# Four edits to a hybrid attention and PEER kernel: a warm-up on GpSimd, a later place for three row gathers, another order of products at two beginnings, residual rows in eight pieces

## The reference

```
proj = x @ w_in                                # GLA and retention inputs
mix  = concat(gla(proj), retention(proj)) @ w_out
h    = layer_norm(ALPHA * x + mix) * ln1_g + ln1_b
q    = h @ w_peer_q                            # 8 heads x 2 x 128
scores = q . subkeys ; top 16 of 128, twice ; top 16 of the 256 sums
act  = gelu(h . u[expert]) * softmax(gate)     # 128 experts a token
out  = layer_norm(ALPHA * h + sum(act * v[expert])) * ln2_g + ln2_b
```

## Time and profile before

| what | value |
|---|---|
| median of 3 runs | 1937.12 us (1935.56 to 1940.14) |
| the profiled execution | 1930.02 us, its span 1928.2 us |
| mean granted TensorE clock | 0.997 |
| PE busy | 1902.5 us, 99% |
| DVE, ACT, POOL busy | 1340.2, 989.5, 1436.9 us |
| DMA moved | 440.60 MB, mean 229 GB/s |

### The profile page before, as it was taken

How to read it: one execution, slowest core, us unless ns; L and a number is a source line. 1 busy time by engine, 2 the same in 40 slices (tenths; PEclk the granted TensorE clock), 3 DMA queues, 4 the chain that set the end, 5 groups by cost and what they waited for, 6 DMA issues and landing times.

```text
span 1928.2 us, 34656 instructions
## 1 busy us (share of the span) xinstructions
PE 1902.5 (99%) x10830; PEld 1664.7 (86%) x10830; DVE 1340.2 (70%) x2305; ACT 989.5 (51%) x1518; POOL 1436.9 (75%) x962
## 2 busy tenths in 40 slices
PE   9999999999999999999999999999999999999996
PEld 8999888888998888888888888888788888888885
DVE  1844012214688877765889998997788888888887
ACT  5544434435445556657455555555555555555553
POOL 6877878887878899989788878786476576666631
PEclk9999999999999999999999999999999999999998
DMA  9555657577869888787977777777899999999983
GB/s 302 174 153 164 205 149 226 176 232 181 212 148 206 185 190 192 166 189 182 251 172 176 173 172 174 167 177 208 305 328 339 333 329 343 357 352 367 359 311 114
DMA packets 197497, 440.60 MB, mean 229 GB/s; under 512 B 29408, under 2 KB 40544, under 8 KB 196272
## 3 DMA queue, kind: packets, MB, share of 16 engines
q1 hardware_dynamic: 181712, 384.40, 69.6%
q0 software_dynamic: 14416, 50.61, 7.6%
q10 hardware_dynamic: 1296, 4.65, 0.7%
HBM read 426.79 MB, written 12.78 MB: 228 GB/s over the span
## 4 chain that ended last, share of the span: by engine, by line
PE 78%; POOL 10%; issue 7%; DMA 3%; DVE 1%; ACT 1%; POOLq 0%; SPq 0%; DVEq 0%; ACTq 0%
PE ps L1817 27%; PE ps L1772 17%; PE ps L1773 9%; PE ps L1512 7%; PE ps L1514 7%; PE ps L1513 7%; POOL u_lo L1429 6%; POOL w_lo L1391 4%; PE ps L1754 3%; DMA v_raw<-in_peer_v 2%; DMA u_raw<-in_peer_u 1%; PE ps L1628 1%; PE ps L1737 0%; DVE u_t L1055 0%; PE ps L1508 0%
## 5 line engine op out<-in xcount | busy, mean ns | idle before, releaser
L1429 POOL TENSOR_TENSOR u_lo<-u_t,u_hi 128x512 fp32r<-128x512 f32 x512 | 653.8, 1300 | 127.5 <-ACT u_hi L637 125.2
L1772 PE MATMUL ps<-xT,u_hi 128*128 128x512 f32 x2048 | 724.3, 397 | 0.6 <-POOL u_lo L1429 0.4
L1773 PE MATMUL ps<-xT,u_lo 128*128 128x256 f32 x2048 | 572.9, 280 | 0.0
L1391 POOL TENSOR_TENSOR w_lo<-raw,w_hi 128x1024 fp32r<-128x1024 f32 x174 | 431.2, 2493 | 99.6 <-ACT w_hi L506 93.2
L637 ACT ACTIVATE u_hi<-u_t 128x512 fp32r<-128x512 f32 x512 | 321.2, 632 | 349.8 <-DVE u_t L1055 348.6
L1772 PEld LDWEIGHTS ps<-xT,u_hi 128*128 128x128 f32 x2048 | 384.2, 188 | 88.2 <-issue 0.9
L1055 DVE STREAM_TRANSPOSE u_t<-u_raw 128x512 f32<-128x512 f32 x512 | 355.5, 702 | 97.5 <-PE ps L1773 60.5
L1773 PEld LDWEIGHTS ps<-xT,u_lo 128*128 128x128 f32 x2048 | 386.7, 189 | 0.0
L506 ACT ACTIVATE w_hi<-raw 128x1024 fp32r<-128x1024 f32 x175 | 184.9, 1059 | 273.7 <-PE ps L1514 261.1
L1454 POOL DMA_INDIRECT sp_rows<-in_peer_v,sp_at x128 | 180.1, 1407 | 152.8 <-DVE far_sum L1268 133.3
L1817 PE MATMUL ps<-v_lo,m_hi 128*128 128x512 f32 x882 | 270.2, 375 | 0.0
(11 more groups left out here) (233 smaller groups left out, 2688.3 us busy)
## 6 DMA issues: line engine op xcount, KB each, us to landing
u_raw<-in_peer_u SPq DMA_DIRECT2D x512, 256.0 KB, 4.8
v_raw<-in_peer_v SPq DMA_DIRECT2D x252, 512.0 KB, 6.2
raw<-in_w_in SPq DMA_DIRECT2D x111, 512.0 KB, 3.8
raw<-in_w_out SPq DMA_DIRECT2D x32, 512.0 KB, 4.8
raw<-in_w_peer_q SPq DMA_DIRECT2D x128, 128.0 KB, 4.3
act_dram<-act_w ACTq DMA_DIRECT2D x4, 1024.0 KB, 6.6
act_dram<-far_act SPq DMA_DIRECT2D x62, 64.0 KB, 5.0
x_again<-in_x SPq DMA_DIRECT2D x1, 2048.0 KB, 8.1
```

The lines of the kernel that those rows point to most:

```text
L1391: pool.tensor_tensor(w_lo[:, k, :], raw[:, k, :], w_hi[:, k % HI_RING, :].bitcast(F32), ALU.subtract).then_inc(lo_done, 1)
L1429: pool.tensor_tensor(u_lo[:, r, :], u_t[:, r, :], u_hi[:, r, :].bitcast(F32), ALU.subtract).then_inc(ulo_done, 1)
L1772: pe.matmul(acc, u_hi[:, r, c], xT[:, :, kt, :], start=kt == 0, stop=False)
L1773: ins = pe.matmul(acc[:, 0:T], u_lo[:, r, c], xT_hi[:, kt, :], start=False, stop=kt == KT - 1)
```

## The change

- **GpSimd**: ahead of the two powers of the last norm, a drain, a multiplication of one column (128x1), a drain and an addition of one column, into a cell that nobody reads.
- **Row gathers**: two (`S_AHEAD`) stand ahead of the activations' gathers instead of five; the other three stand behind the nine `act_gather` of the first chunk.
- **First norm (group 18)**: the first two rows `kt` are turned into two banks. ACT writes each straight to `xT_hi` with gain and bias, and then both again to bank 4, from which DVE makes `xT_lo`. TensorE makes one more turn, then the products high x high and low x high of both rows (`upper_four`), then turns 2 and 3, then the products with `xT_lo` (`lower_four`).
- **Head (group 0)**: `upper_four` of row 0, turn 1, `lower_four` of row 0, and both of row 1.
- **Residual rows**: the two multiplications and two additions are cut in two each, and each of the eight pieces waits for one more step of group 19, `used(O_END + 1, 0)` to `used(O_END + 1, 7)`. `h1_made` is counted behind the sixth and the eighth piece.

```diff
--- before.py
+++ after.py
@@ -53,6 +53,7 @@
 S_CHUNK, S_FIRST = (5, 4), 2
 S_PAIR = sum(S_CHUNK)
 S_SLOTS = S_CHUNK[0]
+S_AHEAD = 2
 S_PAIRS = P // S_PAIR
 LN2_TURN = P // 4 - 1
 UR = 6
@@ -226,6 +227,7 @@
         last_e = small[:, 184:200]
         shift = small[:, 184:186]
         gmax = small[:, 184:200]
+        pool_spare = small[:, 199:200]
         LOW_ROW = 32
         STACK = LOW_ROW + RANK
         wup_sb = wup[0:STACK, :]
@@ -245,6 +247,9 @@
 
         def by_four(row):
             return row.rearrange("p (q t) -> p q t", t=4)
+
+        def first_bank(k):
+            return bank(2 if k else 4)[:, 0:T]
 
         def u_bank(i):
             return bank((0, 1, 7)[i % 3])
@@ -261,6 +266,7 @@
 
         step_free, hi_done, lo_done, acc_free = sem("step_free"), sem("hi_done"), sem("lo_done"), sem("acc_free")
         tr_done, tr_hi, tr_lo = sem("tr_done"), sem("tr_hi"), sem("tr_lo")
+        first_tr, first_hi = sem("first_tr"), sem("first_hi")
         glrw_hi, glrw_lo, glr_done, glrT_done, logit_done = (sem(n) for n in ("glrw_hi", "glrw_lo", "glr_done", "glrT_done", "logit_done"))
         logsig_act, b_done, decay_act, decay_d, decay_done = (sem(n) for n in ("logsig_act", "b_done", "decay_act", "decay_d", "decay_done"))
         lvl_diff, lvl_exp, lvl_ready, lvl_mm, lvl_acc = (sem(n) for n in ("lvl_diff", "lvl_exp", "lvl_ready", "lvl_mm", "lvl_acc"))
@@ -495,6 +501,15 @@
                 act.activation(z, z, ACT.Identity, bias=ln_rows[:, 1, kt:kt + 1], scale=ln_rows[:, 0, kt:kt + 1])
             act.drain()
             act.activation(xT_hi[:, 2 * c:2 * c + 2, :].rearrange("p a b -> p (a b)"), bank(4 + c % 4), ACT.Copy).then_inc(tr_hi, 1)
+
+        def act_first_turn(act):
+
+            for k in range(2):
+                act.wait_ge(first_tr, k + 1)
+                act.activation(xT_hi[:, k, :], first_bank(k), ACT.Identity, bias=ln_rows[:, 1, k:k + 1], scale=ln_rows[:, 0, k:k + 1]).then_inc(first_hi, 1)
+            for k in range(2):
+                ins = act.activation(bank(4)[:, k * T:(k + 1) * T], first_bank(k), ACT.Identity, bias=ln_rows[:, 1, k:k + 1], scale=ln_rows[:, 0, k:k + 1])
+            ins.then_inc(tr_hi, 1)
 
         @block.scalar
         def _(act):
@@ -606,7 +621,8 @@
                 act.wait_ge(sk_mm, c + 1)
                 act.activation(skT[:, 4 * c:4 * c + 4, :].rearrange("p a b -> p (a b)"), bank(4 + c), ACT.Copy).then_inc(sk_sb, 1)
             act.wait_ge(ln1_in, 128)
-            for c in range(4):
+            act_first_turn(act)
+            for c in range(1, 4):
                 act_scaled_turn(act, c)
             for k in range(4, STEPS):
                 hi_steps(O_END, (k,))
@@ -1035,10 +1051,16 @@
 
             dve.wait_ge(ln1_rows_in, 64)
             for a in range(TT):
-                dve.tensor_tensor(part(h1_rows[:, a, :], 0, KT), in_perm(n_perm[:, a, :], 0, KT), part(ln1g_sb[:], 0, KT), ALU.mult)
+                for f in (0, KT // 2):
+                    dve.wait_ge(step_free, used(O_END + 1, 2 * a + f // 8))
+                    dve.tensor_tensor(part(h1_rows[:, a, :], f, KT // 2), in_perm(n_perm[:, a, :], f, KT // 2), part(ln1g_sb[:], f, KT // 2), ALU.mult)
             dve.drain()
             for a in range(TT):
-                dve.tensor_tensor(h1_rows[:, a, :], h1_rows[:, a, :], ln1b_sb[:], ALU.add).then_inc(h1_made, 1)
+                for h in range(2):
+                    c = slice(h * D // 2, (h + 1) * D // 2)
+                    dve.wait_ge(step_free, used(O_END + 1, 4 + 2 * a + h))
+                    ins = dve.tensor_tensor(h1_rows[:, a, c], h1_rows[:, a, c], ln1b_sb[:, c], ALU.add)
+                ins.then_inc(h1_made, 1)
 
 
             def u_quarter(ii, j, f, three=False):
@@ -1459,13 +1481,15 @@
             pool.wait_ge(near_out, 64)
             pool.wait_ge(picks_in, 16)
             pool.wait_ge(uparts_free, UR + 4 * P)
-            for k in range(S_SLOTS):
+            for k in range(S_AHEAD):
                 row_gather(k)
             for s in range(2):
                 pool.wait_ge(far_out[s], 16 * P // 4)
             pool.dma_start(sp_gate[:], gate_dram).then_inc(gate_in, 16)
             for k in range(S_PAIR):
                 act_gather(k)
+            for k in range(S_AHEAD, S_SLOTS):
+                row_gather(k)
             for k in range(S_SLOTS, P):
                 row_gather(k)
                 if k - S_SLOTS + S_PAIR < P:
@@ -1483,6 +1507,10 @@
                 pool.drain()
                 pool.tensor_tensor(o, o, ln2b_sb[:, c], ALU.add).then_inc(y_pool, 1)
 
+            pool.drain()
+            pool.tensor_tensor(pool_spare, sp_gate[:, 0:1], sp_gate[:, 1:2], ALU.mult)
+            pool.drain()
+            pool.tensor_tensor(pool_spare, sp_gate[:, 0:1], sp_gate[:, 1:2], ALU.add)
             ln_power(3, slice(0, 1))
             last_gain(0, 2, 1)
             ln_power(4, slice(1, 2))
@@ -1541,6 +1569,22 @@
                                         kt == 0 and n % 2 == 0, kt == KT - 1, lint=True)
                     ins.then_inc(step_free, 1)
 
+            def upper_four(g, kt):
+
+                for w in (w_hi, w_lo):
+                    for n in range(4):
+                        c = slice(kt * COL + n * P, kt * COL + (n + 1) * P)
+                        o = ps[:, 2 * (g % 2) + n // 2, (n % 2) * T:(n % 2 + 1) * T]
+                        pe.matmul(o, w[:, 0, c], xT_hi[:, kt, :], start=kt == 0 and w is w_hi and n % 2 == 0, stop=False, skip_group_check=True)
+
+            def lower_four(g, kt):
+
+                for n in range(4):
+                    c = slice(kt * COL + n * P, kt * COL + (n + 1) * P)
+                    o = ps[:, 2 * (g % 2) + n // 2, (n % 2) * T:(n % 2 + 1) * T]
+                    ins = pe.matmul(o, w_hi[:, 0, c], xT_lo[:, kt, :], start=False, stop=False, skip_group_check=True)
+                return ins
+
             def steps_t(g, ks=range(STEPS)):
 
                 for k in ks:
@@ -1577,7 +1621,17 @@
             pe.wait_ge(keep_in, 16)
             ready = lambda c: (x_in[c // 2] if c else x_half, 16)
             turn(x_sb, 0, 0, *ready(0))
-            for k in range(STEPS):
+            acc_wait(0)
+            pe.wait_ge(lo_half, 1)
+            pe.wait_ge(tr_hi, 1)
+            upper_four(0, 0)
+            turn(x_sb, 0, 1, *ready(1))
+            pe.wait_ge(tr_lo, 1)
+            lower_four(0, 0)
+            pe.wait_ge(lo_done, 1)
+            upper_four(0, 1)
+            lower_four(0, 1).then_inc(step_free, 1)
+            for k in range(1, STEPS):
                 pe.wait_ge(tr_lo, k + 1)
                 if k < 2:
                     steps_n(0, (k,), between=lambda: turn(x_sb, 0, k + 1, *ready(k + 1)))
@@ -1724,7 +1778,30 @@
             pe.wait_ge(acc_free, freed(O_END))
             keep_busy(bank(0)[:, 0:T], xT_hi[:, KT - 1, :], 8)
             pe.wait_ge(sk_sb, 4)
-            turned_group(O_END, steps_n, n_perm, 2, lambda c: (n_block, 2 * c + 2 if c < 2 else 2 * (c // 2) + 4), lead=4)
+            blocks = lambda c: (n_block, 2 * c + 2 if c < 2 else 2 * (c // 2) + 4)
+            pe.wait_ge(*blocks(0))
+            for k in range(2):
+                for a in range(TT):
+                    ins = pe.transpose(first_bank(k)[:, a * P:(a + 1) * P], by_tile(n_perm, a, k), ident)
+                ins.then_inc(first_tr, 1)
+            pe.sem_inc(tr_done, 1)
+            turn(n_perm, 2, 1, *blocks(1))
+            pe.wait_ge(lo_done, STEPS * O_END + 1)
+            for kt in range(2):
+                pe.wait_ge(first_hi, kt + 1)
+                upper_four(O_END, kt)
+            for c in (2, 3):
+                turn(n_perm, 2, c, *blocks(c))
+            pe.wait_ge(tr_lo, 17)
+            for kt in range(2):
+                ins = lower_four(O_END, kt)
+            ins.then_inc(step_free, 1)
+            turn(n_perm, 2, 4, *blocks(4))
+            for k in range(1, STEPS):
+                pe.wait_ge(tr_lo, 16 + k + 1)
+                steps_n(O_END, (k,))
+                if k + 4 < 8:
+                    turn(n_perm, 2, k + 4, *blocks(k + 4))
 
             def query_scores(n):
 
```

## The result

The changed kernel takes **1948.24 us** (median of 6 runs, 1944.63 to 1953.60), the kernel before 1935.89 beside it (1933.08 to 1940.14). The ratio is 1.0063, 95% interval 1.0049 to 1.0077: 12.3 us slower. The forecast was 1946.5, a step of +9.4 from a median of 1937.1.

What follows compares the result with a forecast made beforehand. The prediction took the kernel to be bound by TensorE's own work. Stand +13.1, clock +2.4, values -2.0 and tail -4.1 gave +9.4, added to the median 1937.1: 1946.5 us, range 1940 to 1954.

Steps and rivals of the forecast that it cites:

- Residual rows and their queue: Before group 20: last piece waits for group 19's end, delaying store and loads; TensorE stands 15.1, ends 13.1 later.
- Rival A: Residual rows are not held, pieces run under group 18 and the store is early: 1929.0, faster; chance 0.07.
- GpSimd's wait gone: Group 19, about 493: eight pieces of 1.2 each remove TensorE's wait of 0.7 for GpSimd's w_lo.
- The clock: In the new stand before group 20, TensorE's clock falls from 2.4 to 1.2 GHz, costing 2.4.
- rival D: Clock doesn't fall in the stand before group 20, or comes back sooner: 1944.1; chance 0.09.
- The cover of 2.4 at DVE: DVE's routing starts 18 late, TensorE 13 to 16; the second wait of its kind, 2.4, covers the rest.
- Norm: First norm, group 18: ACT writes xT_hi directly, so upper products start sooner; gain 1.2.
- Start: Group 0: upper products start earlier but transposes wait for x's second part; step 0 ends at 10.7; gain 0.1.
- Values: Expert values' beginning, about 1357: three row gathers leave the full DMA stretch, removing TensorE's 1.70 stall; gain 2.0.
- Rival C: The value phase gives its gain of 2.0 back, its DMA engines staying above 0.9: 1948.5; chance 0.12.
- Tail: After the last matmul: GpSimd's warm-up moves the 4.19 idle before its first addition into earlier waiting; gain 4.1.
- Rival B: The 4.19 idle in the tail is the drain behind a power, which the change keeps: 1950.6; chance 0.26.

Runs made afterwards that it cites:

- the kernel with ScalarE's store: Kernel before plus new norm order, three rows behind, pieces gated four steps earlier, one drain as warm-up, h1_rows store issued by ScalarE: 1925.95 us against 1932.46.
- the kernel with whole rows: Changed kernel with residual rows made as before, in two multiplications and two additions without waits for group 19: 1927.58 us against 1933.40 for the kernel before.

## Why the prediction was right

The main step held: the last piece waits for the end of group 19, the store for it, and the loads of group 20 for the store. The number is nearer than the working. 1946.5 lies 1.7 below what was measured, but the forecast step was +9.4 and the measured one +12.3 (+9.5 to +14.9 by the interval); 1.2 of the 2.9 between them were hidden because the kernel before came out at 1935.9 and not at 1937.1. That was luck. Point by point, by its own steps:

- **Residual rows and their queue: right.** Issue at 508.5 forecast, 510.3 in the trace; ScalarE's first load of group 20 at 518.85 forecast, 521.25 in the trace; stand 15.1 forecast, 16.0 measured. The 1.8 by which the store was late is the start, which came out 1.9 late where I had a gain of 0.1; the other 0.6 is the load, which took 10.9 behind the store and not 10.3. Alone the pieces cost 17.7, and taking them back returns 18.1 (12.3 + 5.8). Rival A (rows not held) is out.
- **GpSimd's wait gone: right**, 0.9 against 0.7. The pieces took 1.7 to 3.0 beside GpSimd and 1.23 only once it stood idle; I had 1.2 for all. The sum did not suffer, because only the last one counts, and that one is alone. The Trainium skill (SBUF — State Buffer, section SBUF: two separate sides) says that of a DVE operation with two inputs in SBUF and a GpSimd operation that reads SBUF, whichever starts first locks the other out for its whole instruction. 1.23 alone against 3.3 beside GpSimd, in the kernel with ScalarE's store, agrees.
- **The clock: right in size, wrong in kind.** 2.7 against 2.4, and rival D (no fall) is out. But a sum of terms overstates it: with the clock held up, TensorE waited 3.3 for `u_lo` instead, since DVE's routing was as late. The cover of 2.4 at DVE, which I named for the stand, was used up: DVE waits for scores once in the changed kernel (13.0), and twice before (14.8).
- **Norm: right**, 1.1 against 1.2. It has worth only if GpSimd keeps up, which by itself it does not.
- **Start: wrong by 2.0** in the trace, by some 0.9 on average. The step that failed is "step 0 ends at 10.7, as before". I took the landing of `x` as 8.3 from one row; the transposes that need it started between 8.1 and 9.4. Before, twelve products covered that spread; now eight stand ahead of it, and the wait of up to 1.6 was followed in four traces by transposes and products at half the clock (four transposes in 1.11 instead of 0.66). Two more traces have such transposes without the wait.
- **Values: right at their beginning** (2.5 against 2.0; the part alone is 2.5 faster in time, within 0.2 to 3.7). Rival C (it is given back) is not settled.
- **Tail: near in size, wrong in cause.** 3.4 against 4.1: the idle went from 4.19 to 0.16, and the first addition now overlaps DVE's last pieces and takes 1.82 instead of 1.26. In six other traces the gain is 2.4, as there the step "so it is not the later one", of DVE's last piece, fails: it was worked out with DVE undisturbed. But "if they belong to the first add (or the first drain) of the program": it is the first drain behind the gathers. The warm-up worked because a drain stood in it at the right place. Rival B, in which the drain behind a power keeps its cost, is refuted too, as the same drain behind the same power takes 0.65. The Trainium skill's figure of about 6 us for a first call (GPSIMD Engine Reference, section Instruction dispatch) doesn't apply: in the kernel without the warm-up's addition, the first addition of the program came 0.16 behind its drain.

The rest of the ledger is at least in part the execution, not the change. From 700 to 800 TensorE did fewer matmuls in the changed kernel than in the kernel with whole rows, at the same granted clock, never idle:

```profile
700.00:800.00 100.00, 100.00 (x567) 86.76 (x566) 76.81 (x118) 60.53 (x112) 90.16 (x73) 1.00 0.79 184
```

```profile
700.00:800.00 100.00, 100.00 (x579) 87.48 (x578) 78.73 (x115) 64.41 (x118) 92.94 (x75) 1.00 0.82 189
```

That pace of 2% less, worth 3.3 by 850, turned up in 4 of 14 traces: the changed kernel, the one without the addition, the one with the store on ScalarE, and the one with the three rows alone. No edit is common to these and absent from the others. In all four it is one and the same stretch, from some 655 to 825 of the kernel before, with an even 0.19 in each 10 us; what sets it stays open. Take this out of the 19.9, and 16.6 are left; take out the 5.3 of the values too, and it is 11.3, near the 12.3 of the medians. But that the 5.3 are the execution is not shown: it is what rival C is about.

## What to carry to other kernels

When work is spread out behind a counter, look not at its own engine but at who waits for its end: list every customer of the last piece (here a store and the loads queued behind it, a copy that holds up weights, and the right to overwrite the buffer), and work out when each starts to hurt. A recovered stall is worth only as much as the next engine is ahead; subtract the same matmul of two traces before adding terms up. And when a warm-up removes an idle time, take its instructions out one by one before naming the cause.

## What the hardware showed that I had not expected

- The first drain of GpSimd behind a long row of indirect gathers takes 4.68 even some 50 us after the last. Issued with the last gather it takes 9.0 to 10.8 and ends 2.06 behind that gather's landing; the drain in the tail then takes 0.65. A drain ahead of the gathers takes 1.4 and doesn't help.
- TensorE's clock can fall in a gap of only 2.9. In seven traces with a gap ahead of group 20 it fell 1.9 to 5.0 us after the last matmul, differently from run to run, and stayed at one half for 3 to 6 us after TensorE had started again.
- One stretch of 170 us has two paces, 567 or 579 matmuls in the same 100 us, at the same granted clock of 1.00: the slower one in 4 of 14 traces.
